# Top-2 expert layer with experts sorted by load: four of 128 slots one at a time, four of 64 slots two at a time as fp32 products in column halves

## The reference, cut to what matters

```python
def moe_swiglu(h, router, w1, w3, w2):
    logits = (h @ router).astype(jnp.float32)
    top_vals, top_idx = lax.top_k(logits, TOP_K)          # TOP_K = 2
    top_w = jax.nn.softmax(top_vals, axis=-1)
    combine = jnp.sum(jax.nn.one_hot(top_idx, N_EXPERTS, dtype=jnp.float32) * top_w[..., None], axis=-2)
    y = jnp.zeros(h.shape, jnp.float32)
    for e in range(N_EXPERTS):                            # 8; w1, w3: 1024x3584, w2: 3584x1024
        y = y + combine[..., e:e + 1] * swiglu(h, w1[e], w3[e], w2[e]).astype(jnp.float32)
    return y.astype(h.dtype)
```

## Time and profile before

| | |
|---|---|
| three runs, median | 1467.68 us (1466.27 to 1468.15) |
| profiled execution, span | 1471.1 us (no other time of it is given) |
| PE, DVE, ACT, POOL busy | 98%, 81%, 63%, 4% of the span |
| granted TensorE clock, mean | 0.995 |
| first matmul of the first expert | 491.08 us |
| pieces of expert weights | 336 of 1 MiB |
| bytes moved | 426.62 MB, 290 GB/s over the span |

### The profile page before, as it was taken

One profiled execution on the slowest core, in us unless ns is written; L12 is line 12 of the kernel. 1 busy time (PEld: TensorE's weight loads), 2 busy tenths in 40 slices (PEclk: granted clock), 3 DMA queues, 4 the chain that ended last, 5 costly groups with the idle time before them and its releaser, 6 DMA issues.

```text
span 1471.1 us, 18960 instructions
## 1 busy us (share of the span) xinstructions
PE 1447.4 (98%) x7380; PEld 1189.1 (81%) x7380; DVE 1188.1 (81%) x1109; ACT 932.8 (63%) x878; POOL 60.4 (4%) x70
## 2 busy tenths in 40 slices
PE   7999999999999999999999999999999999999998
PEld 6864999998765888888888888888888888888886
DVE  5995545447995788988898898888889888889887
ACT  4273343434373777777777777777777777777774
POOL 1042000000141000000000000000000000000000
PEclk9999999999999899999999999999999999999999
DMA  7750755532822799999999999999999999999993
GB/s 245 231 170 34 253 188 185 172 115 89 278 94 82 274 363 375 369 363 354 339 364 369 376 351 365 370 336 364 369 369 363 356 371 330 365 376 364 367 368 132
DMA packets 203853, 426.62 MB, mean 290 GB/s; under 512 B 7410, under 2 KB 48626, under 8 KB 203764
## 3 DMA queue, kind: packets, MB, share of 16 engines
q1 hardware_dynamic: 202448, 424.90, 80.6%
q10 hardware_dynamic: 1316, 0.49, 0.1%
HBM read 424.31 MB, written 1.05 MB: 289 GB/s over the span
## 4 chain that ended last, share of the span: by engine, by line
PE 87%; DVE 11%; issue 1%; ACT 1%; DMA 1%; ACTq 0%; POOL 0%; DVEq 0%
PE bank L1922 14%; PE bank L1924 14%; PE bank L1923 14%; PE bank L1944 7%; PE bank L1946 7%; PE bank L1945 7%; DVE arena L990 6%; PE bank L1826 3%; PE bank L1828 3%; PE bank L1827 3%; PE bank L1655 2%; PE bank L1456 2%; PE bank L1932 2%; PE bank L1843 1%; PE bank L1844 1%; PE bank L1845 1%
## 5 line engine op out<-in xcount | busy, mean ns | idle before, releaser
L961 DVE TENSOR_TENSOR w_split<-ring,w_split 128x2048 fp32r<-128x2048 f32 x369 | 843.7, 2290 | 192.6 <-ACT w_split L585 191.0
L585 ACT CAST w_split<-ring 128x2048 fp32r<-128x2048 f32 x369 | 706.0, 1914 | 295.6 <-PE bank L1924 161.6
L1922 PE MATMUL bank<-w_split,xe_hi 128*128 128x512 f32 x896 | 355.0, 396 | 0.0
L1924 PE MATMUL bank<-w_split,xe_lo 128*128 128x512 f32 x896 | 349.7, 390 | 0.0
L1923 PE MATMUL bank<-w_split,xe_hi 128*128 128x512 f32 x896 | 348.9, 389 | 0.0
L1924 PEld LDWEIGHTS bank<-w_split,xe_lo 128*128 128x128 f32 x896 | 168.2, 188 | 36.3
L1922 PEld LDWEIGHTS bank<-w_split,xe_hi 128*128 128x128 f32 x896 | 168.3, 188 | 34.9 <-DVE w_split L961 1.2
L1923 PEld LDWEIGHTS bank<-w_split,xe_hi 128*128 128x128 f32 x896 | 168.5, 188 | 33.2
L1944 PE MATMUL bank<-w_split,actT_hi 128*128 128x512 f32 x448 | 175.2, 391 | 0.0
L1946 PE MATMUL bank<-w_split,actT_lo 128*128 128x512 f32 x448 | 174.5, 389 | 0.0
L1945 PE MATMUL bank<-w_split,actT_hi 128*128 128x512 f32 x448 | 174.4, 389 | 0.0
(11 more groups left out here) (239 smaller groups left out, 1424.1 us busy)
## 6 DMA issues: line engine op xcount, KB each, us to landing
ring<-in_moe_w SPq DMA_DIRECT2D x336, 1024.0 KB, 5.8
ring<-in_dense_w SPq DMA_DIRECT2D x33, 1024.0 KB, 5.4
ring<-in_w_in SPq DMA_DIRECT2D x8, 1024.0 KB, 9.5
ring<-in_w_in SPq DMA_DIRECT2D x4, 2048.0 KB, 8.2
ring<-in_w_out SPq DMA_DIRECT2D x4, 2048.0 KB, 7.9
ring<-in_cmp_k_w SPq DMA_DIRECT2D x2, 2048.0 KB, 14.0
ring<-in_cmp_v_w SPq DMA_DIRECT2D x2, 2048.0 KB, 9.3
ring<-in_w_in SPq DMA_DIRECT2D x2, 1120.0 KB, 12.5
```

Of the source, the lines that this page charges most:

```text
L585: nc.scalar.copy(split_part(0, t), raw(t)).then_inc(w_hi_ready, 1)
L961: V.tensor_tensor(split_part(1, t), raw(t), split_part(0, t).bitcast(F32), ALU.subtract).then_inc(w_lo_ready, 1)
L1922: T.matmul(dst, xe_hi[:, kk, own], hi[:, k, :], start=(kk == 0), stop=False)
L1924: last = T.matmul(dst, xe_lo[:, kk, own], hi[:, k, :], start=False, stop=(kk == KD - 1))
```

## The change

Experts are ranked by their number of tokens, with expert 0 always first. The order of work is six units: ranks 0 and 1 (128 slots each, as before), ranks 4 and 5 together (64 slots each), ranks 2 and 3 (128 slots), ranks 6 and 7 together. SP reads the experts' numbers from `order_i`. In a unit of two small experts the pieces of both alternate in the stream, 84 in all; they aren't split, PE reads them from the ring as fp32, and the ring slot is free when PE has used it. Expert a's outputs take partitions 64a to 64a + 63 of the banks. The tokens are `xs` = `xe_hi` + `xe_lo`, added by DVE. All loops over units are unrolled; a second pass runs if one of ranks 0 to 3 has over 128 tokens or another over 64. The core of the diff:

```diff
+    SMALL = CAP // 2
+    BIG_UNIT, SMALL_UNIT = ("big",), ("small",)
+    KIND = (BIG_UNIT, BIG_UNIT, SMALL_UNIT, BIG_UNIT, BIG_UNIT, SMALL_UNIT)
+    COLUMN = (0, 1, 4, 2, 3, 6)
...
+        def freed(u, m):
+            n = PIECES[0][u] + m - RAW
+            v = max(o for o in range(UNITS) if PIECES[0][o] <= n)
+            if KIND[v] is BIG_UNIT:
+                return w_lo_ready, nth(v, SPLITS, BASE + n - PIECES[0][v] + 1)
+            return w_used, BASE + n + 1
...
-            stream_expert(0, 0, True)
-            with sp.Fori(1, E) as j:
-                stream_expert(j, j, False)
+            def expert_at(column):
+                return sp.value_load(order_i[0:1, column:column + 1], min_val=0, max_val=E - 1)
+            def stream_small(u):
+                w = [weights(expert_at(COLUMN[u] + a)) for a in range(2)]
+                for m, (kind, c, half) in enumerate(expert_stream):
+                    for a in range(2):
+                        sp.wait_ge(*freed(u, 2 * m + a))
+                        fetch(w[a], 2 * m + a, kind, c, half)
+            stream_big(0)
+            sp.wait_ge(order_ready, 1)
...
+            def small_pair(u):
+                def small_actT(c):
+                    sc.wait_ge(actT_psum, nth(u, CHUNKS, c + 1))
+                    nc.scalar.copy(actT[:, c % 2, :], bank[4][:]).then_inc(small_actT_ready, 1)
+                scaled_high(u)
+                for c in range(FCH):
+                    sc.wait_ge(w_used, nth(u, PIECES, BASE + 2 * xplace["e1", c, 1] + 2))
+                    silu(u, c)
+                    if c >= 1:
+                        small_actT(c - 1)
+                    if c == 3:
+                        own_slots(u)
+                small_actT(FCH - 1)
...
-            link(V.tensor_tensor(pos_tab[:, :, 0:E], r_(8),
-                                 bank[POS_BANK][:, 0:NT * E].rearrange("p (i e) -> p i e", i=NT), ALU.add))
+            link(V.scalar_tensor_tensor(out=key[:], in0=bank[POS_BANK][:, COUNT0:COUNT0 + E], scalar=float(E), in1=tie[:],
+                                        op0=ALU.mult, op1=ALU.add))
+            V.tensor_tensor(r_(9), r_(8), bank[POS_BANK][:, 0:NT * E].rearrange("p (i e) -> p i e", i=NT), ALU.add)
+            link(V.tensor_tensor(above[:], key[:].unsqueeze(1).to_broadcast([P, E, E]),
+                                 key[:].unsqueeze(2).to_broadcast([P, E, E]), ALU.is_gt))
+            link(V.tensor_reduce(rank[:], above[:], AX_X, ALU.add))
+            link(V.tensor_tensor(perm[:], rank[:].unsqueeze(1).to_broadcast([P, E, E]),
+                                 rank_at[:].unsqueeze(2).to_broadcast([P, E, E]), ALU.is_equal))
+            def in_order(dst, src):
+                for i in range(NT):
+                    link(V.tensor_tensor(moved[:, i], perm[:], src[:, i].unsqueeze(1).to_broadcast([P, E, E]), ALU.mult))
+                link(V.tensor_reduce(dst, moved[:], AX_X, ALU.add))
+            in_order(pos_tab[:, :, 0:E], r_(9))
...
+            in_order(wgt_tab[:, :, 0:E], wgt_tab[:, :, E:2 * E])
+            link(V.tensor_tensor(above[:], perm[:], eidx[:, 0].unsqueeze(1).to_broadcast([P, E, E]), ALU.mult))
+            link(V.tensor_reduce(order_f[:], above[:], AX_X, ALU.add))
+            link(V.tensor_scalar(order_f[:], order_f[:], float(E), None, ALU.add))
+            V.tensor_copy(order_i[:], order_f[:]).then_inc(order_ready, 1)
...
+            def whole_tokens(u):
+                for half in range(2):
+                    dv.wait_ge(xe_ready, nth_pair(u // PAIR, (half + 1) * QB))
+                    part = slice(None), slice(4 * half, 4 * half + 4), slice(u % PAIR * CAP, (u % PAIR + 1) * CAP)
+                    V.tensor_tensor(xs[:, 4 * half:4 * half + 4, :], xe_hi[part].bitcast(F32),
+                                    xe_lo[part].bitcast(F32), ALU.add).then_inc(xs_ready, 1)
+            def small_pair(u):
+                if u % PAIR == 0:
+                    whole_tokens(u)
+                scaled_low(u)
+                for c in range(FCH):
+                    gated(u, c, nth(u, PIECES, BASE + 2 * xplace["e3", c, 1] + 2))
+                    if c == 0:
+                        add_back(u)
...
+            def small_pair(u):
...
+                def up(kind, c):
+                    b = (0 if kind == "e1" else 2) + c % 2
...
+                    for half in range(2):
+                        if kind == "e1" and c == 0:
+                            pe.wait_ge(xs_ready, nth(u, XS_ADDS, half + 1))
+                        w = arrived(kind, c, half, 4)
+                        for k in range(4):
+                            kk = 4 * half + k
+                            for a in range(2):
+                                mm = T.matmul(bank[b][half_slots(a), :], xs[:, kk, half_slots(a)], w[a][:, k, :],
+                                              start=(kk == 0), stop=(kk == KD - 1))
+                                if k == 3:
+                                    mm.then_inc(w_used, 1)
...
+                        for n in range(NH):
+                            for a in range(2):
+                                mm = T.matmul(bank[5 + n][half_slots(a), :],
+                                              actT[:, c % 2, f0 + a * SMALL:f0 + (a + 1) * SMALL],
+                                              w[a][:, k, n * BANK:(n + 1) * BANK], start=start, stop=end)
```

More of the change, by code:

```diff
@@ new lines, in stream_big @@
+                    fetch(w, m, kind, c, half)
+            def stream_small(u):
[6 more added lines that the diff above has]
+            sp.wait_ge(order_ready, 1)
+            for unit in range(1, UNITS):
+                if KIND[unit] is BIG_UNIT:
+                    stream_big(unit)
+                else:
+                    stream_small(unit)
@@ new lines, in _ @@
+            sp.wait_ge(trips_ready, 1)
+            more = sp.value_load(trips_i[0:1, 0:1], min_val=0, max_val=PASS)
+            with sp.If(more > 0):
+                sp.wait_ge(w_used, BASE + PIECES[0][UNITS])
+                with sp.Fori(0, E) as j:
+                    w = weights(j)
+                    for m, (kind, c, half) in enumerate(expert_stream):
+                        sp.wait_ge(w_lo_ready, j * XS + (BASE + SPLITS[0][UNITS] + m - RAW + 1))
+                        fetch(w, m, kind, c, half)
@@ L868, in pair_of_experts @@
                         high_part(BASE + done, j)
                         done += 1
[L870 to L875 removed]
+                        if done == xplace["e3", 0, 0] + 1:
+                            scaled_high(j)
@@ new lines, in _ @@
+            for unit in range(UNITS):
+                if KIND[unit] is BIG_UNIT:
+                    big_expert(unit, (unit + 1) // PAIR if unit % PAIR and unit + 1 < UNITS else None, unit == 0)
+                else:
+                    small_pair(unit)
+            more = dv.value_load(trips_i[0:1, 0:1], min_val=0, max_val=PASS)
+            with dv.If(more > 0):
+                dv.wait_ge(selT_psum, UNITS)
+                for h in range(PAIR):
+                    chosen_slots(E + h, slice(h * CAP, (h + 1) * CAP))
+                with dv.Fori(0, PASS) as pair:
+                    big_expert((pair, 0), None)
+                    big_expert((pair, 1), pair + 1)
@@ new lines, in own_slots @@
+            def own_slots(pair, own, columns):
+                pe.wait_ge(sel_ready, selected(pair))
+                for i in range(NT):
+                    T.transpose(bank[7][:, i * P:(i + 1) * P], sel[:, i, own].bitcast(F32), ident[:])
+                width = CAP // len(columns)
+                for i in range(NT):
+                    for a, column in enumerate(columns):
+                        last = T.matmul(bank[7][a * width:(a + 1) * width, S:S + 1],
+                                        sel[:, i, own.start + a * width:own.start + (a + 1) * width].bitcast(F32),
+                                        wgt_tab[:, i, bass.ds(column, 1)], start=(i == 0), stop=(i == NT - 1))
+                last.then_inc(selT_psum, 1)
@@ new lines, in _ @@
+            for unit in range(UNITS):
+                if KIND[unit] is BIG_UNIT:
+                    big_expert(unit, unit // PAIR, unit % PAIR, COLUMN[unit], (unit + 1) // PAIR if unit % PAIR and unit + 1 < UNITS else None,
+                               unit == 0)
+                else:
+                    small_pair(unit)
+            pe.wait_ge(trips_ready, 1)
+            more = pe.value_load(trips_i[0:1, 0:1], min_val=0, max_val=PASS)
+            with pe.If(more > 0):
+                pe.wait_ge(sel_ready, SEL_AT[TURNS] + NT * PAIR)
+                pe.wait_ge(act_ready, UNITS * FCH)
+                pe.wait_ge(selT_ready, UNITS * 2)
@@ L2007 @@
+                pe.wait_ge(xe_ready, (TURNS + PASS + 1) * (2 * QB))
+            scatter((more, 0))
 def kernel(**inputs):
```

547 lines of the change are left out of this document (308 added, 239 removed).

## The result

The changed kernel takes **1439.38 us** (median of four runs, 1438.94 to 1441.81) against 1466.97 for the kernel before beside it (1465.02 to 1468.15): ratio 0.9816, 95% interval 0.9802 to 0.983. That is 27.6 us faster, 6.4 us above the forecast of 1433 and inside its range. The page of the changed kernel, span 1440.1 us: busy engines, clock and DMA by slices, and the head of the chain that ended last.

What follows compares the result with a forecast made beforehand. PE was taken to bound the kernel, with DMA close behind. Expert stage 972.5 to 929.3 us gave -43, additions +8.7, net -34.5 from a median of 1467.7: 1433 us, range 1412 to 1457.

Steps and rivals of the forecast that it cites:

- The price of a piece: Small units: DMA time for 1 MiB when PE doesn't hold it back, 2.75 us, between 2.65 and 2.90.
- the estimate of 1461 us: Whole kernel if HBM transfers are bound by about 358 GB/s per core, 2.93 us a piece; the prediction doubted it.
- Rival A: Expert stage: DMA gives no more than now, 2.90 us a piece, big units stall; 1457 to 1460 us, chance 0.09.
- C: Rival for small units: seven open requests leave no DMA dips, 2.60 us a piece; 1410 us, chance 0.07.
- First pair 242.8: Expert stage: the first big pair was taken to last 242.8 us, the same as before.
- as long as now: Second big pair, units 3 and 4: taken as unchanged, two big ones between at 244.5 us.
- 2 us for dips: Start of the big pair behind the first small unit: DMA dips stall PE until its lead returns, 2 us.
- PE's wait into unit 3: From small to big unit: PE idles 3.7 us until the first big piece is cast and subtracted.
- The additions of `whole_tokens`: Before the first small pair's first matmul: two DVE additions of 0.68 us each, partly covered; 1 us.
- the chain of eight operations: Router, ranking experts between pos_psum and select(0): eight linked operations 0.21 us apart, 1.7 us, all of it counted.
- only move: Router: two count matmuls of 8 columns were taken to change place only, with no cost given.
- Rival B: Small pairs: PE's clock halves and stays, 301 us a pair, PE-bound; 1593 us, chance 0.07.

Runs made afterwards that it cites:

- in_place: The changed kernel with tie and rank_at in unused rows of rt, not new tensors, so later tensors keep their earlier addresses; 1421.34 us, ratio 0.9703.
- fill: in_place plus 13 fp32r matmuls without use behind the last product of the first small unit; 1422.81 us, ratio 0.9693.
- experts64: The kernel before with an unused 64 bytes a partition right ahead of xe_hi, moving only expert-stage tensors; 1488.81 us.
- experts128: The kernel before with an unused 128 bytes a partition right ahead of xe_hi, moving only expert-stage tensors; 1492.78 us.
- half_bytes: The changed kernel with only half of each small-unit piece loaded, work of PE, ACT and DVE the same; 1308.2 us.
- shift64: The kernel before with an unused tensor of 64 bytes a partition behind eidx, where the changed kernel adds tie and rank_at; 1494.6 us, ratio 1.0205.
- experts256: The kernel before with an unused 256 bytes a partition right ahead of xe_hi, moving only expert-stage tensors; 1468.1 us.
- small_last: in_place with the units in the order big, big, big, big, small, small; 1425.48 us, ratio 0.9709.
- shift128: The kernel before with an unused tensor of 128 bytes a partition behind eidx; 1493.95 us.
- serial_halves: The changed kernel with all products of a piece pair's first expert ahead of the second's, instead of alternating; 1441.61 us.

## Why the prediction was right, and where it wasn't

**The mechanism was right.** Small units are bound by the transfer of their 84 pieces, with PE waiting 56 us in unit 2 and ACT and DVE nearly idle; half the bytes take the bound away. Column halves run beside each other. PE's own work is 152.5 us, where I had 157. The chain that ended last has DMA for 21% of the span, where I had named some 30%: between two transfers of 12.04 us it runs through 3.67 us of PE's matmuls, and I had counted the small units as DMA alone.

**The price of a piece was mis-sized.** The forecast took 2.75 us (381 GB/s); the windows show 393 to 395 GB/s once the queue is full, 2.67 us: 12.1 + 76 x 2.67 = 215, and PE's work in unit 2 ended after 215.7 us. So a unit is 5 us shorter than 221. The dips of the trace before (323 GB/s at worst), for which I had added 0.1 us to the best 2.65, are not there: the stretches of 40 us within unit 2 have 393 GB/s or more. The figure of about 358 GB/s per core of the Trainium skill (DMA: Bandwidth & Descriptors, section "Where 436 GB/s comes from") doesn't bind here, as these windows show. The same page, section "Measured (HBM→SBUF, 128 partitions, SWDGE, issued from GpSimd)", has it as the share of each core when both cores of a memory domain stream. This kernel runs on one core, and no run here shows the other case; so the estimate of 1461 us took a figure for another case. Rival A is out (unit 2 would have been 232), C had the direction.

**"First pair 242.8", and units 3 and 4 "as long as now", failed.** This is the step that failed: the big pairs together cost 502.1 us, where the sum had 489.3 with its 2 us for dips. The change part by part never asked where its two new tensors lie, and so put the price of a big matmul at 0.227 us as before; it was 0.233. The runs showed 64 bytes to be worth 11.9 us in the big pairs, and 6.4 in the dense stage between the profiled executions of the changed kernel and `in_place`. The sign of being wrong named beforehand, units 3 and 4 longer by more than 5 us, came: 9.0 us, of which `in_place` takes 6.4 away. The first pair grew by 5.8. In the sum this loss (12.8) nearly cancels against the cheaper small units (446.7 with their extras forecast, 435.2 measured): the near hit of the expert stage, -35.2 for -36.5, is in part luck. Without the shift the change is worth 44.5 us, 3.0%, not 1.8%.

**Seams.** PE's wait into unit 3 was 3.2 us for 3.7. Where I had 2 us of dips there came 2.7 us of half clock (14 matmuls at 0.43 instead of 0.233); in `in_place`, with a shorter stretch of it, `fill` got back 0.6 us of the big pair by keeping the clock up. The additions of `whole_tokens` cost nothing that can be seen, for 1. The router cost 2.5 for 2 between the two profiled executions: the chain of eight operations took the 1.7 us it was given. The other 0.9 is a step I had at nothing: the two count matmuls, of which I wrote that they "only move", now stand ahead of the position matmuls, and DVE waits 1.10 us for PE's results where it waited 0.24. SP's queue has 0% of the chain, as forecast.

**The profiled execution of before was not a usual one.** It had 13.7 us at half clock in the router and a mean granted clock of 0.995; the nine executions of before beside `in_place` had 0.998 or 0.999. In `experts64` and `experts128`, with the same router, the clock was at half for 3.4 and 6.8 us there and the stage took 16.2 and 17.5 us, not 18.7. Against such an execution the changed kernel's 21.2 us is 3.7 to 5.0 us more, not 2.5; this is an estimate, since no profile of a usual execution of before was taken. I had also set the span of 1471.1 beside a median of times as 3.4 over it. In every run on record the time is 1.7 to 1.9 us above the span of the same execution, so that execution took about 1472.8 us, some 6 above the median of 1466.97.

**Rival B didn't come.** In the changed kernel's two small units the clock fell once, for 3.4 us, though PE stopped for 0.9 to 1.8 us behind almost every 3.65 us of matmuls. That fall, at 1248.6 us, came 0.4 us behind a wait of 2.58; another of 2.36 brought none. `in_place` had two such falls in unit 5. The Trainium skill (TensorE: Matmul & The Clock Gate, section "HAM oscillation — how this bites in real kernels") tells of bursts that each began at half clock behind a wait for DMA, and its waits were longer than its bursts; that is not repeated here. The one wait of 3.2 us, behind unit 2, did bring half clock. A kernel whose waits equal its bursts wasn't tried.

## What to carry to other kernels

When a change adds a tensor, however small, look where it is allocated: time the kernel before with the same bytes added and nothing else. Compare the start-to-start distance of one kind of matmul before and after, since PE reads as fully busy either way. A stage that has been close behind the bound can be priced by the rate of its queue when full, not by its mean rate under the old bound; and a filler that keeps the clock up is worth only what isn't hidden by the next wait. Before a shorter stage is put down to an edit, look at the same stage in kernels whose code is the same up to there: the router's took 18.2 us in `half_bytes` and 21.2 in the changed kernel, which have the same code there.

## What the runs showed of the hardware

- With everything else equal, fp32r products of 512 columns were 0.227 us apart, or 0.232 to 0.233 when the stationary operand was moved by 64 or 128 bytes a partition; moved by 256 they were at 0.227. The mean length of a weight load in the records was 188 ns both in the kernel before and in `experts64`. Where the bytes collide was not found.
- Gate and up products of the dense stage, with 256 columns, whose moving operand was the one shifted, were 0.120 us apart with 64 bytes (`shift64`, the changed kernel). Without, they were 0.113 in some executions (`in_place`, `experts64`, `experts256`) and 0.118 in others (before, `experts128`, `small_last`), at the same addresses.
- With one router, that of before, the clock was at half for 3.4 us (`shift64`, `experts64`), 6.8 (`shift128`, `experts128`) or 13.7 (before, `experts256`) on the way to the first expert matmul.
- One core alone kept 395 GB/s for 200 us (393 to 395 in most slices of the page), with transfers of 1 MiB.
- fp32 half products of 64 stationary and 512 moving columns in different column halves started within 0.1 us of each other, 672 of 672 pairs (the changed kernel); where the program puts eight records of one half ahead of the other's, still 382 of 672 (`serial_halves`).
